# Gated linear attention inside a one-core block: level factors multiplied in place, small levels scored on 32x32 diagonal blocks under one mask, differences taken in pairs, loop written out

## The chip, the cores and the metric

The kernel runs on one core of a Trainium2 chip. A core has TensorE (PE in the profile; PEld is its weight load), VectorE (DVE), ScalarE (ACT), GpSimd (POOL) and SyncE (SP), which run side by side and meet at semaphores. The metric is the device time of one execution in microseconds. The kernel before takes 3309.83 us, the median of 3 runs (3308.33 to 3311.6).

## The reference, cut to what matters

The program is a whole model block (projections, an RWKV-7 mixer, a gated linear attention mixer, an output projection, two feed-forward parts). The change touches the gated linear attention of 4 heads (64 key channels, 128 value channels each) over 1024 tokens, once forward and once backward in time:

```python
def gla_chunked(q, k, v, log_a):
    bc = jnp.cumsum(to_chunks(log_a), axis=-2)
    def step(S, inp):
        o_inter = jnp.einsum('bhcd,bhde->bhce', q_c * jnp.exp(b_c), S)
        diff = b_c[:, :, :, None, :] - b_c[:, :, None, :, :]
        dmat = jnp.exp(jnp.where(mask, diff, -jnp.inf))
        scores = jnp.einsum('bhid,bhjd,bhijd->bhij', q_c, k_c, dmat)
        o_intra = jnp.einsum('bhij,bhje->bhie', scores, v_c)
        S = (S * jnp.exp(b_last[:, :, 0, :])[..., None]
             + jnp.einsum('bhcd,bhce->bhde', k_c * jnp.exp(b_last - b_c), v_c))
        return S, o_inter + o_intra
...
    o_f = gla_chunked(q_h, k_h, v_h, heads(log_a[:, :, 0], GLA_DK))
    o_b = flip(gla_chunked(flip(q_h), flip(k_h), flip(v_h), flip(heads(log_a[:, :, 1], GLA_DK))))
    o = (o_f + o_b).transpose(0, 2, 1, 3)
```

The product over channels with a different decay for every pair of tokens is what makes the scores costly.

## The kernel before

The kernel works on blocks of 128 tokens (BLK), 8 of them (NBLK), with channels on partitions: two tiles of 128 channels (index i) hold two heads each (index par, rows 0 to 63 and 64 to 127). `gla_decay` (L667) writes the running sums of log decays, `sums`, for both directions; `gla_mix` (L735) does the attention; `gla_finish` (L1021) normalises. Each is a block with a barrier at its end.

Inside a block the decay between two tokens is split by the level at which they part: for the levels s = 1, 2, 4, ..., 64 (LEVELS, 7 of them) tokens of one half of a pair of runs of length s look at tokens of the other half, and both are referred to the boundary between them. For a level `level_diff` (L944) writes four differences on DVE (L953 to L956, 128x128 elements each), `level_exp` (L814) exponentiates 128x512 on ACT (L819), DVE multiplies with q and k (L1009), PE forms all four 128x128 score matrices (`scores`, L884, 64 rows of contraction), DVE multiplies them by the 128x128 mask of the level (`masked`, L965), and POOL adds them up (L848, L852). The diagonal is an eighth score. After the last sum PE multiplies with the values (`outputs_of_block`, L893) and DVE adds to `y` (`add_outputs`, L981). The state between blocks runs beside that for both directions: `outputs_of_state` (L907, and the gain at L914) and `next_state` (L975).

All five engines run a loop over the 8 blocks. DVE begins a turn with copies into fixed tiles (L988 to L997) and starts it only when its own last turn and PE's are done, so no work of block j+1 is on DVE, ACT or PE before the outputs of block j are added. Order within an engine is the order of the code; there is no scheduler. Two score buffers and two of each level buffer (`n % 2`) tie level n to level n-2.

Of the kernel before, what the change touches and what calls it, by code (L numbers as in the profile page):

```python
# [34 lines left out]
P = 128  # L35
# [32 lines left out]
for _name, _n in VEC_FIELDS:  # L68
# [7 lines left out]
                ("block_keep", 16), ("gla_diag", 1), ("gla_level", 7)]  # L76
# [11 lines left out]
def constants():  # L88
# [28 lines left out]
    for n, s in enumerate(LEVELS):  # L117
        out[:, CONST["gla_level"] + n] = (p // (2 * s) == j // (2 * s)) & (p // s != j // s)
    out[:, CONST["gla_diag"]] = 2.0 * (p == j)
# [547 lines left out]
def gla_decay(core, dram_const, dram_a_up, lora, sums):  # L667
# [5 lines left out]
    with ExitStack() as ctx:  # L673
# [5 lines left out]
        loaded, products, act_did, dve_did = (core.sem(f"gd_{x}") for x in ("loaded", "products", "act", "dve"))  # L679
# [35 lines left out]
        def _(dve):  # L715
            dve_made.begin(dve)
            dve.wait_ge(loaded, 32)
# [17 lines left out]
def gla_mix(core, dram_const, z, sums, y, room):  # L735

    nc = core.nc
    levels = range(7)  # L740
    scored = ["diag"] + [f"level{n}" for n in levels]
    with ExitStack() as ctx:
# [5 lines left out]
        used = [0]  # L748

        def both(name, tiles, a=1):  # L750

            at = used[0]
            used[0] += tiles * BLK
            own = sb(name, [P, tiles * BLK])[:, :]
            views = (own, room[:, at:at + tiles * BLK])
            if a == 1:
                return [x.rearrange("p (i t) -> p i t", t=BLK) for x in views]
            return [x.rearrange("p (a i t) -> p a i t", a=a, t=BLK) for x in views]

        mask = sb("mask", [P, 8, BLK])  # L760
        summed = sb("summed", [P, 2, 2, BLK])
        summed_d = both("summed_d", 2)
        qk = both("qk", 4, 2)
        v = both("v", 4)
        diff_s = both("diff_s", 4, 2)
        grown_s = both("grown_s", 4, 2)
        qk_s = both("qk_s", 4, 2)
        v_tok = both("v_tok", 4)
        k_tok = both("k_tok", 2)
        state = both("state", 2)  # L770
        diff = sb("diff", [P, 2, 2, 2, BLK])
        grown = sb("grown", [P, 2, 2, 2, BLK])
        qk_l = sb("qk_l", [P, 2, 2, 2, BLK])
        part = sb("part", [P, 2, 4, BLK])
        score = sb("score", [P, 4, BLK])
        ps_score = psum("score", [P, 2, 2, 512])
        ps_v = psum("v", [P, 4, BLK])
        ps_k = psum("k", [P, 4, BLK])
        ps_o = psum("o", [P, 2, 512])
        loaded, zeroed, y_zeroed = core.sem("gm_loaded"), core.sem("gm_zeroed"), core.sem("gm_y_zeroed")  # L780

        def state_steps(d):
            return [f"state0_{d}", f"state1_{d}"]

        def y_steps(d):
            return [f"y0_{d}", f"y1_{d}"]
        dve_steps = ["q_0", "block_sums", "summed_0", "diff_s_0", "q_1", "summed_1", "diff_s_1", "diff_level0"]
        dve_steps += ["qk_s_0", "qk_s_1"]
        for n in levels:
            dve_steps += ([f"diff_level{n + 1}"] if n < 6 else []) + [f"qk_level{n}", f"part_{scored[n]}"]  # L790
            dve_steps += {2: state_steps(1) + y_steps(1), 5: state_steps(0)}.get(n, [])
        dve_steps += ["part_level6"] + y_steps(0)
# [4 lines left out]
        dve_made = Marks(core.sem("gm_dve"), dve_steps)  # L797
        act_made = Marks(core.sem("gm_act"), act_steps)
        pool_made = Marks(core.sem("gm_pool"), [f"sum_{r}" for r in scored[1:]])
        pe_made = Marks(core.sem("gm_pe"), pe_steps)  # L800
        block = ctx.enter_context(nc.Block())

        def tokens(d, j):
# [2302 lines left out]
```

## Time and profile before

| | us |
|---|---|
| median of 3 runs | 3309.83 |
| the profiled execution | 3310.85 |
| its span | 3309.1 |
| of it `gla_mix`, barrier to last add | 248.45 |
| one turn of its loop, from one L988 to the next | 30.3 |
| TensorE busy over the whole span | 91% |
| TensorE busy inside `gla_mix` | 54% |
| DVE busy inside `gla_mix` | 81% |

A line of the timeline gives the start, the duration, the engine, the line, what is written from what, and in brackets how long the engine was idle before and what released it. A duration holds some latency: the next instruction of the same engine can start before it is over, so the difference of two starts is what an instruction costs its queue. An fp32 matmul leaves two records for PE and two for PEld; a transpose leaves one. "big" is the buffer that holds z, y and, before the change, the second copy of several tiles.

### The profile page before, as it was taken

How to read it: one execution, taken by the hardware profiler on the slowest of the kernel's cores; microseconds unless marked ns; L12 is line 12 of the kernel's file. 1: busy time of each engine (PE TensorE's matmuls, PEld its weight loads, DVE VectorE, ACT ScalarE, POOL GpSimd, SP SyncE). 2: the span in 40 equal slices, each digit the busy share in tenths (PEclk: the TensorE clock that was granted, in tenths of full speed). 3: DMA queues.
4: the chain of work that ended last, by engine and by line, in shares of the span. 5: the costliest groups of instructions: out<-in, count | busy, mean ns of one | idle time of the engine just before them, and what ended most of it. 6: DMA issues, size and time to landing. Idle time of an engine off the chain costs nothing.

```text
span 3309.1 us, 55091 instructions
## 1 busy us (share of the span) xinstructions
PE 2995.7 (91%) x23744; PEld 2447.9 (74%) x23744; DVE 1543.4 (47%) x2265; ACT 1169.4 (35%) x1887; POOL 357.9 (11%) x375
## 2 busy tenths in 40 slices
PE   6955559988888879999999999999999999999997
PEld 5844447767787738788888888778787888888886
DVE  4638875433454445443334332666545443334323
ACT  4653335532222124432233232543224333233322
POOL 1003231225444220000000000000000000000000
PEclk8976659998999879999999999999999999999998
DMA  3410004422110013222222223222232222223222
GB/s 125 140 46 0 0 7 154 140 97 57 33 42 14 18 62 103 87 92 96 95 96 90 95 96 108 83 89 89 90 101 83 96 96 96 96 96 121 96 96 82
DMA packets 99137, 273.36 MB, mean 83 GB/s; under 512 B 8160, under 2 KB 35168, under 8 KB 98784
## 3 DMA queue, kind: packets, MB, share of 16 engines
q1 hardware_dynamic: 90128, 237.52, 22.0%
q0 software_dynamic: 8784, 32.51, 2.9%
q8 instruction: 181, 2.97, 0.4%
q14 instruction: 44, 0.36, 0.0%
HBM read 257.42 MB, written 12.58 MB: 82 GB/s over the span
## 4 chain that ended last, share of the span: by engine, by line
PE 59%; DVE 2%; ACT 1%; issue 0%; DMA 0%; DVEq 0%; ACTq 0%
PE be_ps L2696 43%; PE be_ps L2717 14%; PE be_ps L2730 1%; DVE be_ring L2486 1%; PE be_ps L2438 0%; PE be_ps L2432 0%; ACT be_whi L2763 0%; DVE be_raw_r L2869 0%; DMA be_raw<-in_ple_gate 0%; DVE be_total L2451 0%; DVE ext_r L2496 0%; ACT big L2769 0%; DVE big L2459 0%; DVE big L2468 0%; ACT be_ring L2393 0%
## 5 line engine op out<-in xcount | busy, mean ns | idle before, releaser
L2869 DVE TENSOR_TENSOR be_raw_r<-be_raw,be_whi 128x1024 fp32r<-128x1024 f32 x361 | 442.3, 1225 | 993.2 <-ACT be_whi L2763 993.0
L2696 PE MATMUL be_ps<-ext_r,be_whi 128*128 128x512 f32 x2304 | 715.5, 392 | 15.2 <-PEq L2106 8.6
L2763 ACT CAST be_whi<-be_raw 128x1024 fp32r<-128x1024 f32 x361 | 378.8, 1049 | 873.9 <-DMA be_raw<-in_ffn_down 316.3
L2696 PE MATMUL be_ps<-big_r,be_whi 128*128 128x512 f32 x2048 | 642.8, 395 | 2.4 <-DVE big_r L2494 2.4
L2696 PEld LDWEIGHTS be_ps<-ext_r,be_whi 128*128 128x128 f32 x2304 | 433.3, 189 | 108.3 <-issue 10.2
L2696 PEld LDWEIGHTS be_ps<-big_r,be_whi 128*128 128x128 f32 x2048 | 383.9, 188 | 96.8 <-DVE big_r L2494 2.8
L2696 PE MATMUL be_ps<-ext_r,be_raw_r 128*128 128x512 f32 x1152 | 449.9, 391 | 0.0
L2696 PE MATMUL be_ps<-big_r,be_raw_r 128*128 128x512 f32 x1024 | 408.3, 399 | 0.0
L2717 PE MATMUL be_ps<-ext_r,be_whi 128*128 128x512 f32 x1152 | 354.6, 389 | 0.0
L2696 PEld LDWEIGHTS be_ps<-ext_r,be_raw_r 128*128 128x128 f32 x1152 | 217.6, 189 | 45.7
L2717 PEld LDWEIGHTS be_ps<-ext_r,be_whi 128*128 128x128 f32 x1152 | 216.3, 188 | 45.0
L2696 PEld LDWEIGHTS be_ps<-big_r,be_raw_r 128*128 128x128 f32 x1024 | 192.5, 188 | 45.1
L2717 PE MATMUL be_ps<-ext_r,be_raw_r 128*128 128x512 f32 x576 | 224.1, 389 | 0.0
L2717 PEld LDWEIGHTS be_ps<-ext_r,be_raw_r 128*128 128x128 f32 x576 | 108.1, 188 | 22.5
L884 PE MATMUL gm_ps_score<-gm_qk_l 64*128 64x128 f32 x448 | 58.5, 405 | 55.4 <-DVE gm_qk_l L1009 55.4
L2674 POOL DMA_DIRECT2D out<-big x1 | 0.9, 852 | 973.8 <-DVE big L2468 973.8
L884 PEld LDWEIGHTS gm_ps_score<-gm_qk_l 64*128 64x128 f32 x448 | 46.4, 281 | 69.2 <-DVE gm_qk_l L1009 66.5
L2797 ACT CAST ext_r<-be_gate 128x512 fp32r<-128x512 f32 x72 | 44.7, 621 | 142.0 <-DVE be_gate L2890 142.0
L1788 PE MATMUL rw_ps<-rw_x,rw_by_beta 64*64 64x32 f32 x2560 | 92.9, 223 | 1.8 <-ACT rw_x L1671 1.4
L1788 PEld LDWEIGHTS rw_ps<-rw_x,rw_by_beta 64*64 64x64 f32 x2560 | 84.8, 139 | 9.1 <-ACT rw_x L1671 5.0
L2671 POOL DMA_DIRECT2D ext<-in_p x2 | 1.4, 710 | 832.8 <-PE be_ps L2717 832.8
L2791 ACT ACTIVATE be_gate<-be_ps 128x512 f32<-128x512 f32 x88 | 52.7, 599 | 97.5 <-PE be_ps L2696 97.3
(342 smaller groups left out, 4261.3 us busy)
## 6 DMA issues: line engine op xcount, KB each, us to landing
be_raw<-in_ffn_gate SPq DMA_DIRECT2D x88, 512.0 KB, 3.3
be_raw<-in_ffn_up SPq DMA_DIRECT2D x88, 512.0 KB, 3.3
be_raw<-in_ffn_down SPq DMA_DIRECT2D x88, 512.0 KB, 3.3
be_raw<-in_conv_in SPq DMA_DIRECT2D x48, 512.0 KB, 3.3
gp_ada<-in_ada POOLq DMA_DIRECT2D x24, 512.0 KB, 3.6
rp_ada<-in_ada POOLq DMA_DIRECT2D x24, 512.0 KB, 3.7
rwkv_prepared<-big SPq DMA_DIRECT2D x16, 512.0 KB, 3.3
be_raw<-in_w_out SPq DMA_DIRECT2D x16, 512.0 KB, 3.4
```

What stands on the lines that cost most here:

```text
L884: mm = pe.matmul(ps_score[:, n % 2, par, i * BLK:(i + 1) * BLK], src[rows, 1, i], src[rows, 0, i], start=True, stop=True)
L1788: return pe.matmul(out, lhs, moving, start=start, stop=True, skip_group_check=True)
L2486: dve.scalar_tensor_tensor(s.ring[:, i % 2], self.h(i), self.gain(i), self.ps[:, 6] if plan.copy is None else s.kept[:, :], ALU.mult, ALU.mult
L2671: pool.dma_start(p_raw[:, :, cols(half)], a["p"][:, :, cols(half)]).then_inc(p_loaded[half], 16)
L2674: pool.dma_start(out[:, :, cols(0)], big[:, 0:KD, cols(0)]).then_inc(stored[0], 16)
L2696: mm = pe.matmul(ps[:, bank], part[:, k * P:(k + 1) * P], xs(k), start=(k == 0 and i == 0), stop=(k == KD - 1 and i == 2))
L2717: mm = pe.matmul(ps[:, m], part[:, m * P:(m + 1) * P], x, start=(j == 0 and i == 0), stop=(j == NF - 1 and i == 2))
L2730: mm = pe.matmul(ps[:, steps.bank[n, g]], part[:, at], x[:, k, cols(half)], start=(k == 0 and i == 0), stop=(k == 1 and i == 2))
L2763: act.copy(w.hi[:, n % 3], w.raw[:, n % 3]).then_inc(w.hi_ready, 1)
L2791: act.activation(s.gate[:, j % 2, 0:HALF], ps[:, steps.bank[n, 0]], ACT.Silu).then_inc(act_took, 1)
L2797: act.copy(inner(f, j)[0], s.gate[:, j % 2, 0:HALF]).then_inc(a_hi_made, 1)
L2869: dve.tensor_tensor(w.lo(n), w.raw[:, n % 3], w.hi[:, n % 3].bitcast(F32), ALU.subtract).then_inc(w.lo_ready, 1)
```

## The change

- The scaling of q by 0.125 moves out of the loop into `gla_decay`: one DVE instruction of 128x2048.
- The loop over blocks is written out. The copies of q, k, v and of the sums into fixed tiles go; one copy of the sums a block stays and moves to ACT. `exp` of the sums is taken straight from `sums`.
- `level_diff` takes both directions in one instruction: two of 128x256 a level instead of four of 128x128. They go into a ring of 5 slots, are exponentiated in place and multiplied in place.
- The levels 1 to 16 and the diagonal are scored only inside 32x32 diagonal blocks: 16 small matmuls each into one PSUM bank per par, 128x768 masked by one DVE instruction, and folded by three POOL instructions (128x384, 128x128, 128x128). The levels 32 and 64 are scored only where they count (16 and 8 small matmuls), need no mask and stay in PSUM; PE adds the folded low part by a product with the identity (`add_low_scores`), ACT copies the whole (`finish_scores`), PE multiplies with the values (`from_block`).
- The outputs of both directions gather in one PSUM tile; in the first half of the blocks ACT copies them to `y`, in the second half DVE adds them. `y` needs no zeroing.
- The end of block j (low part, high copy, values, outputs) is placed inside block j+1 on PE, ACT and DVE.
- The mask that is loaded shrinks from 128x1024 to 128x384.

The diff, cut to its core:

```diff
-            with dve.Fori(0, NBLK) as j:
-                dve.wait_ge(*dve_made.before(j))
-                dve.wait_ge(*pe_made.before(j))
...
+            def level_diff(j, n):
+                s, to_back = LEVELS[n], 2 * BLK
+                own, out = summed[:, j % 2], ring[:, slot(j, n)]
+                q_out, k_out = out[:, 0], out[:, 1]
+                dve.wait_ge(*act_block.by("summed", j))
+                if j * len(LEVELS) + n >= n_ring:
+                    before, level = ring_user(j, n)
+                    dve.wait_ge(*pe_made.by(f"score{level}", before))
+                middle = by_pair(own, s - 1, to_back + 1, s, 0)
+                dve.tensor_tensor(by_pair(q_out, s, -s, s), by_pair(own, s, to_back - s, s), middle, ALU.subtract)
+                dve.tensor_tensor(by_pair(k_out, 0, s, s), middle, by_pair(own, 0, to_back + s, s), ALU.subtract
+                                  ).then_inc(*dve_made(f"diff{n}"))
...
+            def masked(j):
+                dve.wait_ge(*pe_made.by("score4", j))
+                if j:
+                    dve.wait_ge(*pool_made.by("low", j - 1))
+                dve.tensor_tensor(part.rearrange("p a n t -> p a (n t)"), ps_low[:, :, 0:n_low * 2 * sub],
+                                  mask[:, :].rearrange("p (a t) -> p a t", a=1).to_broadcast([P, 2, n_low * 2 * sub]),
+                                  ALU.mult).then_inc(*dve_made("masked"))
+
+            def next_state(j):
+                dve.wait_ge(*pe_made.by("gain", j))
+                dve.wait_ge(*pe_made.by("from_state", j))
...
+            for j in range(NBLK):
                 level_diff(j, 0)
-                for d in range(2):
-                    dve.wait_ge(*act_made.by(f"exp_s_{d}", j))
+                for d in two:
+                    to_end(j, d)
+                level_diff(j, 1)
+                for d in two:
+                    state_factors(j, d)
                 for n in levels:
+                    if n + 2 < len(LEVELS):
+                        level_diff(j, n + 2)
+                    level_factors(j, n)
+                    if n == 3 and j > NBLK // 2:
+                        add_outputs(j - 1)
+                    if n == 4:
+                        next_state(j)
+                masked(j)
```

```diff
+            def low_scores(place, q, k):
+                for i in two:
+                    for b in range(BLK // sub):
+                        own = slice(b * sub, b * sub + sub)
+                        for par in two:
+                            rows = slice(64 * par, 64 * par + 64)
+                            ins = mm(ps_low[own, par, (place * 2 + i) * sub:(place * 2 + i + 1) * sub], k(rows, i, own), q(rows, i, own))
+                return ins
...
+            for j in range(NBLK):
+                value_tokens(j, 0)
+                own_scores(j)
+                if j:
+                    add_low_scores(j - 1)
+                value_tokens(j, 1)
+                key_tokens(j)
                 scores(j, 0)
-                transposes(j, 1)
                 scores(j, 1)
+                if j:
+                    from_block(j - 1)
+                gains(j)
                 scores(j, 2)
-                outputs_of_state(j, 1)
-                for n in range(3, 8):
-                    scores(j, n)
-                    if n == 5:
-                        outputs_of_state(j, 0)
-                outputs_of_block(j)
+                scores(j, 3)
+                from_states(j)
+                scores(j, 4)
+                scores(j, 5)
+                scores(j, 6)
```

```diff
+            pool.tensor_tensor(part[:, :, 0:3], part[:, :, 0:3], part[:, :, 3:6], ALU.add).then_inc(*pool_made("sum3"))
+            pool.wait_ge(*pool_made.by("sum3", j))
+            pool.tensor_tensor(part[:, :, 0], part[:, :, 0], part[:, :, 1], ALU.add).then_inc(*pool_made("sum1"))
+            pool.wait_ge(*pool_made.by("sum1", j))
+            pool.tensor_tensor(low[:, j % 2], part[:, :, 0], part[:, :, 2], ALU.add).then_inc(*pool_made("low"))
```

On DVE, one level of the middle of a block (s = 4) stood like this before. The four L95x rows are the differences of the next level (s = 8), L1009 the product with q and k, L965 the mask:

```order
L965 TENSOR_TENSOR gm_part<-gm_ps_score,gm_mask 128x512 [waits gm_pe]
L953 TENSOR_TENSOR gm_diff<-gm_summed 128x16x8 [waits gm_act]
L954 TENSOR_TENSOR gm_diff<-gm_summed 128x16x8
L955 TENSOR_TENSOR gm_diff<-gm_summed 128x16x8
L956 TENSOR_TENSOR gm_diff<-gm_summed 128x16x8
L1006 REGISTER_ALU
L1009 TENSOR_TENSOR gm_qk_l<-gm_qk,gm_grown 128x512 [waits gm_pe,gm_act]
```

Each level had this shape, with a mask behind its product. After the change DVE has this from the last level of block 0 to the first product of block 1 (L1024 and L1025 are differences, L1033 those to the end of the block for the state, L1039 the state factors, L1044 a level's product, L1050 the only mask):

```order
L1044 TENSOR_TENSOR gm_ring<-gm_ring,big 128x512 [waits gm_act] x2
L1050 TENSOR_TENSOR gm_part<-gm_ps_low,gm_mask 128x768 [waits gm_pe]
L1024 TENSOR_TENSOR gm_ring<-gm_summed 128x2x128 [waits gm_pe,gm_act_block]
L1025 TENSOR_TENSOR gm_ring<-gm_summed 128x2x128
L1033 TENSOR_TENSOR gm_qk_s<-gla_sums 128x256 x2
L1024 TENSOR_TENSOR gm_ring<-gm_summed 128x2x64x2 [waits gm_pe,gm_act_block]
L1025 TENSOR_TENSOR gm_ring<-gm_summed 128x2x64x2
L1039 TENSOR_TENSOR gm_qk_s<-gm_qk_s,big 128x512 [waits gm_act] x2
L1024 TENSOR_TENSOR gm_ring<-gm_summed 128x2x32x4 [waits gm_pe,gm_act_block]
L1025 TENSOR_TENSOR gm_ring<-gm_summed 128x2x32x4
L1044 TENSOR_TENSOR gm_ring<-gm_ring,big 128x512 [waits gm_act]
```

Of eight masks one is left, and the next block's differences follow it directly.

On PE the middle of a block stood like this before (L884 a level's scores, L907 the products with the state, L914 the gain of the state):

```order
L884 MATMUL gm_ps_score<-gm_qk_l 128x128 x3
L901 REGISTER_ALU [waits gm_act]
L907 MATMUL gm_ps_o<-gm_qk_s,gm_state 128x128 [waits gm_dve]
L907 MATMUL gm_ps_o<-gm_qk_s,gm_state 128x128 x3
L914 MATMUL gm_ps_k<-gm_v_tok,gm_k_tok 64x128 x4
L877 REGISTER_ALU
L880 REGISTER_ALU [waits gm_dve]
L884 MATMUL gm_ps_score<-gm_qk_l 128x128 [waits gm_dve]
```

After the change PE begins block 1 like this (L900 values and L909 keys transposed, L892 all other products; the row that writes `gm_ps_high` from `gm_low` is block 0's `add_low_scores`):

```order
L900 MATMUL gm_ps_v<-const,big 128x128 [waits gm_act]
L900 MATMUL gm_ps_v<-const,big 128x128 x3
L892 MATMUL gm_ps_low<-big 32x32 [waits gm_dve]
L892 MATMUL gm_ps_low<-big 32x32 x15
L892 MATMUL gm_ps_high<-gm_low,const 32x2x32 [waits gm_pe,gm_pool]
L892 MATMUL gm_ps_high<-gm_low,const 32x2x32 x7
L900 MATMUL gm_ps_v<-const,big 128x128 [waits gm_act]
L900 MATMUL gm_ps_v<-const,big 128x128 x3
L909 MATMUL gm_ps_k<-const,gm_qk_s 128x128 [waits gm_dve]
L909 MATMUL gm_ps_k<-const,gm_qk_s 128x128 x3
L892 MATMUL gm_ps_low<-gm_ring 32x32 [waits gm_dve]
L892 MATMUL gm_ps_low<-gm_ring 32x32 x15
```

A level is 16 matmuls instead of 4, and the last block's end stands ahead of this block's second transposes, keys and scores. On ACT, block 1 has this (L847 and L818 exponentials, L827 the copy of block 0's scores, L857 and L861 the transposed values and keys out of PSUM, L832 outputs to `y`):

```order
L847 ACTIVATE gm_qk_s<-gm_qk_s 128x256 [waits gm_dve] x2
L818 ACTIVATE gm_ring<-gm_ring 128x512 [waits gm_dve]
L827 COPY big<-gm_ps_high 128x512 [waits gm_pe_out]
L818 ACTIVATE gm_ring<-gm_ring 128x512 [waits gm_dve]
L857 COPY gm_v_tok<-gm_ps_v 128x512 [waits gm_pe] x2
L861 COPY gm_k_tok<-gm_ps_k 128x512 [waits gm_pe]
L818 ACTIVATE gm_ring<-gm_ring 128x512 [waits gm_dve] x2
L832 COPY big<-gm_ps_o 128x2x2x128 [waits gm_pe_out]
```

The copy of the last block's scores now stands between the first and the second level's exponential; before, ACT had nothing of another block in a turn.

## Rows read from the trace of the kernel before

**Rows 1.** Busy time by stage: `gla_mix`, from barrier to last add.
```profile
core 0: us, PE busy (x) PEld busy (x) DVE busy (x) ACT busy (x) POOL busy (x), PEclk, DMA share, GB/s
242.30:490.75 248.45, 134.77 (x928) 106.39 (x928) 201.75 (x498) 80.19 (x144) 79.36 (x57) 0.60 0.01 2
```

**Rows 2.** Timeline of DVE: first instruction, one turn, the last turn's end.
```profile
247.21 0.29 DVE L988 TENSOR_SCALAR gm_qk<-big 128x256 f32 x1 [3.69 <-DMA gm_mask<-in_const]
...
276.86 0.29 DVE L988 TENSOR_SCALAR gm_qk<-big 128x256 f32 x1 [0.25 <-DVE big L981]
...
277.93 0.42 DVE L997 TENSOR_TENSOR gm_diff_s<-gm_summed_d 128x256 f32<-128x256 f32 x1
278.26 0.29 DVE L988 TENSOR_SCALAR big<-big 128x256 f32 x1
...
288.01 0.68 DVE L1009 TENSOR_TENSOR gm_qk_l<-gm_qk,gm_grown 128x512 f32<-128x512 f32 x1
288.62 0.68 DVE L965 TENSOR_TENSOR gm_part<-gm_ps_score,gm_mask 128x512 f32<-128x512 f32 x1
289.22 0.59 DVE L975 SCALAR_TENSOR_TENSOR big<-big,gm_ps_k 128x128 f32<-128x128 f32 x2
289.73 0.74 DVE L981 TENSOR_TENSOR big<-big,gm_ps_o 128x256 f32 x2
...
307.12 0.29 DVE L988 TENSOR_SCALAR gm_qk<-big 128x256 f32 x1 [0.25 <-DVE big L981]
...
485.62 0.69 DVE L965 TENSOR_TENSOR gm_part<-gm_ps_score,gm_mask 128x512 f32<-128x512 f32 x1 [0.90 <-PE gm_ps_score L884]
490.00 0.75 DVE L981 TENSOR_TENSOR big<-big,gm_ps_o 128x256 f32 x2 [3.69 <-PE gm_ps_o L893]
```

**Rows 3.** Groups by line and shape, DVE, 240 to 491 us: busy, mean ns.
```profile
L955 DVE TENSOR_TENSOR gm_diff<-gm_summed 128x128 f32<-128x128 f32 x56 | 38.3, 684 | 0.0
L954 DVE TENSOR_TENSOR gm_diff<-gm_summed 128x128 f32<-128x128 f32 x56 | 15.8, 282 | 0.0
```

**Rows 4.** Timeline of POOL in the same turn: two of its entries.
```profile
286.39 1.35 POOL L848 TENSOR_TENSOR gm_score<-gm_part 128x512 f32<-128x512 f32 x1 [12.81 <-DVE gm_part L965]
...
292.84 3.86 POOL L852 TENSOR_TENSOR gm_score<-gm_score,gm_part 128x512 f32<-128x512 f32 x2 [2.11 <-DVE gm_part L965]
```

**Rows 5.** Groups by line: a POOL sum of 128x256 in the RWKV mixer.
```profile
L1715 POOL TENSOR_TENSOR rw_e_beta<-big,rw_e_beta 128x256 f32<-128x256 f32 x16 | 11.4, 733 | 0.6
```

**Rows 6.** Timeline of ACT in the same turn: exponential, copy out of PSUM.
```profile
280.74 0.61 ACT L819 ACTIVATE gm_grown<-gm_diff 128x512 f32<-128x512 f32 x1
281.26 0.56 ACT L833 COPY gm_v_tok<-gm_ps_v 128x512 f32<-128x512 f32 x1
```

**Rows 7.** Timeline of PE in the same turn: 64-row and 128-row products.
```profile
288.82 0.72 PE L884 MATMUL gm_ps_score<-gm_qk_l 64*128 64x128 f32 x8 [1.74 <-DVE gm_qk_l L1009]
292.21 1.23 PE L884 MATMUL gm_ps_score<-gm_qk_l 64*128 64x128 f32 x8 [2.67 <-DVE gm_qk_l L1009]
...
303.90 2.07 PE L893 MATMUL gm_ps_o<-gm_score,gm_v_tok 128*128 128x128 f32 x8 [2.30 <-POOL gm_score L852]
```

**Rows 8.** Timeline of PE in the RWKV mixer: 32 records of small products.
```profile
756.10 1.13 PE L1788 MATMUL rw_ps<-rw_masks,rw_beta_end 64*64 64x64 f32 x32 [0.91 <-DVE rw_by_kappa L2012]
...
766.01 1.86 PE L1788 MATMUL rw_ps<-rw_mx,rw_xt 64*64 64x32 f32 x32
...
776.86 1.12 PE L1788 MATMUL rw_ps<-rw_x,rw_by_beta 64*64 64x32 f32 x32
778.28 0.69 PE L1788 MATMUL rw_ps<-rw_masks,rw_beta_end 64*64 64x64 f32 x32 [0.29 <-DVE rw_by_kappa L2012]
```

**Rows 9.** Busy time and clock in stretches of 4 us.
```profile
284.00:288.00 4.00, 3.08 (x34) 2.38 (x33) 3.57 (x9) 1.39 (x3) 1.35 (x1) 0.85 0.00 0
...
756.00:760.00 4.00, 2.42 (x68) 2.10 (x72) 0.58 (x1) 1.35 (x4) 3.85 (x6) 0.50 0.00 0
...
776.00:780.00 4.00, 3.71 (x141) 3.48 (x141) 1.88 (x4) 2.46 (x9) 3.20 (x5) 1.00 0.02 4
```

More of the change, by code:

```diff
@@ L116, in constants @@
             out[:, CONST["level_m"] + 2 * n + d] = np.tile(off | (row == col), 4)
[L117 to L119 removed]
+    row, own = p % 32, np.arange(32)[None, :]
+    low = [(row // (2 * s) == own // (2 * s)) & (row // s != own // s) for s in LEVELS[:5]] + [2.0 * (row == own)]
+    out[:, CONST["gla_low"]:CONST["gla_low"] + 3] = np.concatenate([np.tile(x, 2) for x in low], axis=1).reshape(P, 3, P)
     return out.reshape(P, NCONST * P)
@@ L732, in _, with gla_mix @@
                                            ALU.add).then_inc(*dve_made("scan"))
-def gla_mix(core, dram_const, z, sums, y, room):
+def gla_mix(core, dram_const, z, sums, y):
     nc = core.nc
-    levels = range(7)
-    scored = ["diag"] + [f"level{n}" for n in levels]
+    levels = range(len(LEVELS))
+    low_levels, n_low = range(5), 6
+    n_ring, sub = 5, 32
+    two, heads = range(2), range(4)
     with ExitStack() as ctx:
@@ L760, in gla_mix @@
[L760 to L786, printed above, removed]
@@ L918, in _, with mm, value_tokens @@
-            with pe.Fori(0, NBLK) as j:
-                transposes(j, 0)
+            pe_out.begin(pe)
+            def mm(out, lhs, moving, start=True):
+                return pe.matmul(out, lhs, moving, start=start, stop=True, skip_group_check=True)
+            def value_tokens(j, d):
+                if d:
+                    pe.wait_ge(*act_made.by("v_tok0", j))
+                elif j:
+                    pe.wait_ge(*act_made.by("v_tok1", j - 1))
+                for h in heads:
+                    ins = pe.transpose(ps_v[:, h], z[:, 4 + h, tokens(d, j)], cst(core, "ident"))
+                ins.then_inc(*pe_made(f"v_tok{d}"))
@@ new lines, in from_states @@
+            def from_states(j):
+                pe.wait_ge(*(dve_made.by("state", j - 1) if j else (zeroed, 1)))
+                if j:
+                    pe.wait_ge(y_taken, j)
+                for d in two:
+                    for i in two:
+                        for par in two:
+                            rows = slice(64 * par, 64 * par + 64)
+                            ins = mm(ps_o[:, par, d, i], state[rows, d, i], qk_s[rows, j % 2, d, 0, i], start=(d == 0 and i == 0))
+                ins.then_inc(*pe_made("from_state"))
```

366 lines of the change are left out of this document (188 added, 178 removed).

## The prediction

> **What bounds the kernel now.** First the busy time by stage: the changed stage lasts 248.45 us, with DVE busy 201.75, PE 134.77, ACT 80.19 [rows 1]. So DVE is the engine to cost. Then DVE's timeline: a turn goes from 276.86 to 307.12, 30.3 us [rows 2]. In it DVE is hardly idle until the last mask; then nothing runs on it for about 4 us, because POOL's last sum, PE's product and the addition to `y` come one after the other (the 3.69 in front of L981, seen for the last turn at 490.00) [rows 2]. Third, the groups by shape: L954 and L955 are the same 128x128 subtraction, but L955 takes 684 ns on average where L954 takes 282, which is 38.3 - 15.8 = 22.5 us over the stage [rows 3]. POOL's sum at 286.39 starts just then [rows 4]: DVE waits for it. So a turn is DVE's own work, some 3 us and more that POOL takes from it, and the tail.
>
> **The price of DVE's instructions**, taken as the distance between two starts. 256 elements from two SBUF inputs: 278.26 - 277.93 = 0.33. 512 elements: 288.62 - 288.01 = 0.61, with PSUM as a source the same (289.22 - 288.62 = 0.60). 128 elements of the state's form: two in 289.73 - 289.22 = 0.51, so 0.26 each [rows 2]. From 256 to 512 elements costs 0.28, so 768 elements: 0.61 + 0.28 = 0.89, an estimate from these rows.
>
> **Part by part, DVE of one block after the change.** 14 differences of 256 elements, 14 x 0.33 = 4.6. Two differences to the block's end, 0.7. Two state factors and seven level factors of 512, 9 x 0.61 = 5.5. Four state updates, 1.0. One mask, 0.9. Outputs: 2 x 0.61 in half the blocks, 0.6 on average. Sum 13.3. Gone are the copies, seven of eight masks (each 0.60) and 14 instruction starts of the differences. New strides in the paired form are not seen before; I take 0.33. The bounds: the dense price less a saving that no row suggests, and the full price of 512 elements, 0.61, if a stride halved the rate, which would be 14 x 0.28 = 3.9 more; it is nearest to the dense row, since L954, strided as well, takes its usual 282 ns [rows 3].
>
> **POOL.** Instead of seven sums of 512 there are 384, 128 and 128 elements. 512 take 1.35 [rows 4], 256 take 0.73 [rows 5], so 2.4 ns an element: 1.0, 0.45 and 0.45, 1.9 us, with hand-overs 2.3. DVE loses at most these 1.9 (before, 22.5 / 8 = 2.8 at L955 alone); POOL now starts right behind the mask, among the next block's differences, which all read two SBUF tiles. I take 1.7.
>
> **PE of one block.** A matmul is two records. Seven groups of 16 small matmuls (32 records): the nearest rows are 32 records of 64x64 tiles, 0.69 at full clock and 1.13 at half, and 32 records of a slower arrangement, 1.12 and 1.86 [rows 8] (the clocks are those of the stretches around, 1.00 and 0.50, that is 2.4 and 1.2 GHz [rows 9]). So 4.8 to 7.8 at full clock, 7.9 to 13.0 at half. State products and gains are 32 records of 128 columns, 4 x 0.72 or 4 x 1.23; the value products 8 records, 2.07 at half and about 1.2 at full by the ratio of the other two; three sets of four transposes, at most 0.72 or 1.23 each [rows 7]; the identity products and level 64, half a group each, 0.7 to 1.9. In all 11.7 to 15.0 at full clock, 18.6 to 25.7 at half. Which clock? The stretch 284 to 288, with PE busy 3.08 of 4 us, has 0.85, and the dense small products of the RWKV mixer hold 1.00 [rows 9]; the stage's mean is 0.60 [rows 1]. With the work packed into half the time I take full clock for most of it.
>
> **Waits that remain on DVE.** (a) DVE's state update needs PE's state products, which stand behind level 8's scores. From level 8's factors DVE has only a difference pair and a factor to do, 0.66 + 0.61 = 1.27; PE needs a group (0.69 to 1.12) and 16 records (1.44), about 2.4 with hand-overs. Wait 1.1; at half clock up to 1.86 + 2.46 - 1.27 + 0.2 = 3.2. (b) From the mask the last block's end runs: POOL 2.3, identity product 0.5, copy on ACT 0.6, ACT's next exponential and value copy 1.1, transposes on PE 1.4, key copy 0.6, third exponential 0.6, hand-overs 1: about 8.1 until DVE may multiply level 4 (ACT prices [rows 6]). DVE has for that time 5 difference pairs (3.3), 0.7, two state factors and two level factors (2.4), 6.4, and POOL's 1.7: 8.1. It just covers; I leave 0.4. (c) ACT's copies of outputs in front of an exponential, 0.5. What is queued behind each of these waits is the rest of DVE's block, since DVE is in order.
>
> Block: 13.3 + 1.7 + 1.1 + 0.4 + 0.5 = **17.0 us**.
>
> **Head and tail.** Before, DVE waited 3.69 us for the mask's 512 KB and began at 247.21, 4.9 after the stage's start [rows 2]. 192 KB should land earlier; between no wait (1.2) and the same (4.9) I take 3.0. The tail from the last mask to the end was 490.75 - 485.62 = 5.1; now one mask (0.9), POOL 2.3, identity product 0.6, ACT copy 0.6, value products 1.2 to 2.1 and two additions 1.3: 7.2. The scaling of q lies in `gla_decay`, ahead of everything DVE waits for there; even at 2 us it costs nothing on the path. Sum: 3.0 + 8 x 17.0 + 7.2 - 0.7 (the last block's outputs counted twice) = 145.5. Gain 248.45 - 145.5 = 103. Against the profiled execution's 3310.85, which is 1.0 above the median, that gives 3208; the median should come about 3207.5. The stages around touch no line of this and are taken as unchanged.
>
> **A rule about the shared port.** The row: POOL's sum at 286.39 ran at once and held DVE's L955 for its length; but the pair at 292.84 took 3.86 for two sums of 1.35, so POOL itself waited some 1.1 us while DVE went through four instructions [rows 4]. The Trainium skill, page "SBUF — State Buffer", section "Who interferes with whom", says that a DVE instruction with two SBUF inputs and a GpSimd instruction that reads SBUF exclude each other for a whole instruction, and that the one issued first wins. It doesn't say who is served when both stand in line. Both outcomes agree with it; the second is the rival B below.
>
> **Rivals.**
> A. *Everything covers*: small products at 0.69 and no wait on DVE: 13.3 + 1.0 = 14.3, sum 124, 3186. For it: PE at 11.7 is below that. Against: wait (a) does not go away.
> B. *POOL starves*: behind the mask DVE has 3 pairs, two end differences, two state factors, a level factor, in an unbroken run of 5.1 us with two SBUF inputs each. If POOL gets in only when DVE stops for level 2's exponential, chain (b) begins 5.1 later and DVE stands about 3.5 more. Block 20.5, stage 3.0 + 164 + 6.5 = 173.5: 3236. For it the 292.84 pair; against, that most of POOL's entries waited for nothing.
> C. *PE at half clock becomes the bound*: 18.6 to 25.7 a block, plus about 1: stage 166 to 223, so 3229 to 3285. For it the present 0.60; against, that PE was mostly waiting then.
> D. *Slower than before*: matmuls on neighbouring 32-column tiles do not overlap, so that each record pays more than its start. PE issues 2 x 148 + 12 = 308 records a block. Break-even is (248.45 - 9.5) / 8 = 29.9 us a block, 97 ns a record; if each took as long as a 128-column record at half clock, 1.23 / 8 = 0.154 [rows 7], a block would take 47.4 us and the kernel 3310.85 - 248.45 + 8 x 47.4 + 9.5 = 3451. Against it: the slowest small products seen are 1.86 / 32 = 58 ns [rows 8].
> E. *It doesn't do what it says*: the blocks don't overlap because some semaphore of block j+1 waits for block j's outputs. Then chain (b) and the values stand in the open, some 8 us a block more than 17: 25, stage 209.5, 3272. The order of instructions shows no such wait.
>
> **How the numbers follow.** Forecast 0.52 (3196 to 3224); A 0.12; B 0.13; C 0.18; D 0.02; E 0.02; 0.01 for a case within noise. The measurement can tell about 0.2%, 6.6 us. All but D and the last are faster by more. The range 3186 to 3255 takes in A, the forecast, B and the better half of C, and leaves out about 0.15.
>
> **What would show it.** The stage's length near 145 us; distances between two masks near 17; differences at 0.33 apart; the small groups of 16 matmuls between 0.69 and 1.12 at a granted clock near 1; a wait of about 1 us in front of the state updates; POOL's first sum starting within 1 us of the mask (right) or 4 to 5 behind it (B); PE idle less than a tenth at 0.5 (C). The forecast is wrong if the copy of the high scores on ACT comes so late that DVE waits at level 2 or 4 for several us, or if paired differences cost more than 0.4.

## The result, and the profile after

The changed kernel takes **3234.58 us** (median of 4 runs, 3223.78 to 3236.62); the kernel before, on the same chip, 3310.72 (4 runs). The ratio is 0.9764, with a 95% interval of 0.9741 to 0.9786: faster by 2.4%, inside the range of 3186 to 3255, but 26 us above the 3208 that was forecast. The profiled execution took 3234.0, with a span of 3232.2. It stands within 2 us of what rival B gave (3236), and the trace shows B's mechanism.

The busy time by stage, cut where the stage ends (columns as in [rows 1]):

```profile
core 0: us, PE busy (x) PEld busy (x) DVE busy (x) ACT busy (x) POOL busy (x), PEclk, DMA share, GB/s
242.30:410.00 167.70, 86.30 (x2464) 71.29 (x2464) 109.12 (x249) 70.21 (x153) 49.72 (x24) 0.65 0.01 3
```

Against [rows 1], 248.45 us became 168, DVE's 201.75 busy us became 109.12 and PE's 134.77 became 86.30. DVE is busy 65% of the stage, where it was 81%: it stands idle again. POOL is down by 29.6 only, to 49.72 for 24 instructions, and that is the number to stop at: the three sums of a block were priced at 1.9, and they take 6.2 on average.

One block on DVE, from its mask to the next (L1050 is the mask, L1044 a level's product, L1059 the state updates; last column as in [rows 2]):

```profile
299.62 0.95 DVE L1050 TENSOR_TENSOR gm_part<-gm_ps_low,gm_mask 128x768 f32<-128x768 f32 x1
300.49 0.42 DVE L1024 TENSOR_TENSOR gm_ring<-gm_summed 128x256 f32<-128x256 f32 x1
300.82 0.42 DVE L1025 TENSOR_TENSOR gm_ring<-gm_summed 128x256 f32<-128x256 f32 x1
301.15 0.76 DVE L1033 TENSOR_TENSOR gm_qk_s<-gla_sums 128x256 f32<-128x256 f32 x2
...
305.30 0.43 DVE L1025 TENSOR_TENSOR gm_ring<-gm_summed 128x256 f32<-128x256 f32 x1
309.56 0.69 DVE L1044 TENSOR_TENSOR gm_ring<-gm_ring,big 128x512 f32<-128x512 f32 x1 [3.83 <-ACT gm_ring L818]
...
313.21 0.69 DVE L1044 TENSOR_TENSOR gm_ring<-gm_ring,big 128x512 f32<-128x512 f32 x1 [2.29 <-ACT gm_ring L818]
...
316.53 0.69 DVE L1044 TENSOR_TENSOR gm_ring<-gm_ring,big 128x512 f32<-128x512 f32 x1 [0.68 <-ACT gm_ring L818]
318.02 1.12 DVE L1059 SCALAR_TENSOR_TENSOR gm_state<-gm_state,gm_decay,gm_ps_k 128x128 f32<-128x128 f32 x4 [0.81 <-PE gm_ps_o L892]
319.06 1.29 DVE L1044 TENSOR_TENSOR gm_ring<-gm_ring,big 128x512 f32<-128x512 f32 x2
320.27 0.95 DVE L1050 TENSOR_TENSOR gm_part<-gm_ps_low,gm_mask 128x768 f32<-128x768 f32 x1
```

The block is 320.27 - 299.62 = 20.65 us, of which 3.83 + 2.29 + 0.68 + 0.81 = 7.6 are waits; DVE's own work is 13.04, where 13.3 was forecast. From 300.49 to 305.73 DVE never stops. Now POOL beside it, in this block and in the last one, behind which DVE has nothing to do:

```profile
300.65 5.93 POOL L878 TENSOR_TENSOR gm_part<-gm_part 128x384 f32<-128x384 f32 x1 [13.81 <-DVE gm_part L1050]
306.66 0.45 POOL L880 TENSOR_TENSOR gm_part<-gm_part 128x128 f32<-128x128 f32 x1
307.19 0.45 POOL L884 TENSOR_TENSOR gm_low<-gm_part 128x128 f32<-128x128 f32 x1
...
403.37 0.99 POOL L878 TENSOR_TENSOR gm_part<-gm_part 128x384 f32<-128x384 f32 x1 [13.50 <-DVE gm_part L1050]
```

The same sum of 384 elements has a record of 5.93 us in the first seven blocks (5.92 to 5.93 in each) and of 0.99 in the eighth. The sum itself is not slow: it ends 0.85 us after DVE's run ends (306.58 against 305.73), which is about what it takes alone. So it seems to have waited through the run and only then run; the experiments below test that. Behind it the chain is as the prediction had it. First PE, which waits for POOL (`gm_low`), then ACT, in the same block:

```profile
307.70 0.65 PE L892 MATMUL gm_ps_high<-gm_low,const 32*32 32x64 f32 x16 [6.60 <-POOL gm_low L884]
```

```profile
302.27 0.61 ACT L818 ACTIVATE gm_ring<-gm_ring 128x512 f32<-128x512 f32 x1
308.42 0.59 ACT L827 COPY big<-gm_ps_high 128x512 f32<-128x512 f32 x1 [5.53 <-PE gm_ps_high L892]
308.90 0.63 ACT L818 ACTIVATE gm_ring<-gm_ring 128x512 f32<-128x512 f32 x1
```

ACT's copy of the last block's scores is queued ahead of the second level's exponential, so DVE waits for an exponential whose input, the differences at 301.82 and 302.16, it had finished by 302.58, 6.3 us before that exponential starts at 308.90. The list of waits sums it up for the stage (us in total, times, longest):

```profile
PE gm_ps_high L892 <- POOL gm_low L884: 47.9, 8, 6.6
DVE gm_ring L1044 <- ACT gm_ring L818: 45.5, 18, 3.8
DVE gm_state L1059 <- PE gm_ps_o L892: 4.9, 8, 1.3
```

Read alone, the second line says that ACT is late. ACT was waiting for PE, PE for POOL, and POOL for DVE itself: DVE waits for its own unbroken run.

Behind the stage nothing changed by design, but the RWKV mixer's 2560 products took 383.2 us from first to last start against 377.2 before. The eleven kernels of the experiments below, none of which touches them, have 375.2 to 383.6 there, so this is a run's own scatter. The stage gave 80.6 us (the first product behind it starts at 411.6 instead of 492.2); the mixer took 6.0 back and the rest of the kernel gave 2.3, so that the profiled execution shows only 76.9. In the experiments I therefore read the stage by that start, called the marker, first and the total second.

### The profile page after: what moved, and what is told of

Its sections match the earlier page's. It is cut to its first block, busy times and chain, and to the rows that moved or that the text cites. A ratio compares the mean times of both kernels' runs of the same rounds, so it can differ in the third digit from the quotient of the medians.

```text
span 3232.2 us, 57142 instructions
## 1 busy us (share of the span) xinstructions
PE 2949.1 (91%) x25280; PEld 2417.1 (75%) x25280; DVE 1451.8 (45%) x2017; ACT 1159.3 (36%) x1896; POOL 328.1 (10%) x342
## 3 DMA queue, kind: packets, MB, share of 16 engines
q1 hardware_dynamic: 90128, 237.19, 22.4%
## 4 chain that ended last, share of the span: by engine, by line
PE 60%; DVE 2%; ACT 1%; issue 0%; DMA 0%; DVEq 0%; ACTq 0%
PE be_ps L2767 44%; PE be_ps L2788 15%; DVE be_ring L2557 1%; PE be_ps L2801 1%; PE be_ps L2509 0%; PE be_ps L2503 0%; ACT be_whi L2834 0%; DVE be_raw_r L2940 0%; DMA be_raw<-in_ple_gate 0%; DVE be_total L2522 0%; DVE ext_r L2567 0%; ACT big L2840 0%; DVE big L2530 0%; DVE big L2539 0%; ACT be_ring L2464 0%
## 5 line engine op out<-in xcount | busy, mean ns | idle before, releaser
L1477 PE MATMUL rp_acc<-xn_hi,rp_whi 128*128 128x512 f32 x240 | 78.1, 407 | 4.7 <-PEq L1097 4.7
L1859 PE MATMUL rw_ps<-rw_mx,rw_xt 64*64 64x32 f32 x2048 | 77.0, 225 | 4.0 <-DVE rw_mx L2125 1.6
```

The source lines that it names most:

```text
L1477: ins = pe.matmul(acc[:, s % 2, hf * HALF:(hf + 1) * HALF], part[:, s % 2, k], x[:, k, hf * HALF:(hf + 1) * HALF], start=(k == 0 and part ...
L1859: return pe.matmul(out, lhs, moving, start=start, stop=True, skip_group_check=True)
```

## The experiments

The theory: POOL's sum can't start beside a DVE instruction with two inputs in SBUF, and DVE, which always has the next one at hand, is served first. Rivals: the sum is simply slow next to other traffic; ACT's order is at fault; PE is the bound. Each ratio is to the kernel before, measured again in the same series (3304.09 to 3306.7); since that differs from the 3310.72 above, medians of different series are compared by ratio or by the marker. Line numbers shift a little from version to version.

**1. State updates behind the mask.** Their inputs are the state and PE's PSUM, so only one tensor in SBUF.

```diff
-            dve_steps += {4: ["state"], 6: ["masked"]}.get(n, [])
+            dve_steps += {6: ["masked", "state"]}.get(n, [])
...
-                    if n == 4:
-                        next_state(j)
                 masked(j)
+                next_state(j)
```

> Edit: in the changed kernel the four state updates of a block (one SBUF tensor, one PSUM tensor each, 1.04 us together) move from behind level 16's factors to behind the mask; nothing is added or left out. Theory (POOL's first sum of 384 elements takes 5.93 us because it waits until DVE ends its run of instructions with two SBUF inputs): POOL gets in at once, its sum takes about 1.0 us, what hangs on it comes 4.9 us earlier, a block takes 16 to 17.5 us instead of 20.6, and the kernel 3201 to 3215. Rival (the sum is slow for another reason, such as a late release or a slow form of 384 elements): it stays near 5.9 us and the kernel near 3234.

Measured: 3183.45 us (3180.17 to 3185.99), 0.9624 of before [0.9608, 0.964]; the stage is 43.6 us shorter than with the change alone (marker 368.0 against 411.6). DVE and POOL behind a mask:

```profile
313.83 0.96 DVE L1050 TENSOR_TENSOR gm_part<-gm_ps_low,gm_mask 128x768 f32<-128x768 f32 x1 [0.56 <-PE gm_ps_low L892]
314.70 1.11 DVE L1059 SCALAR_TENSOR_TENSOR gm_state<-gm_state,gm_decay,gm_ps_k 128x128 f32<-128x128 f32 x4
315.73 0.42 DVE L1024 TENSOR_TENSOR gm_ring<-gm_summed 128x256 f32<-128x256 f32 x1
316.07 0.67 DVE L1025 TENSOR_TENSOR gm_ring<-gm_summed 128x256 f32<-128x256 f32 x1
...
314.86 1.00 POOL L878 TENSOR_TENSOR gm_part<-gm_part 128x384 f32<-128x384 f32 x1 [13.07 <-DVE gm_part L1050]
315.94 0.52 POOL L880 TENSOR_TENSOR gm_part<-gm_part 128x128 f32<-128x128 f32 x1
```

The sum takes 0.99 to 1.00 us in all eight blocks, the updates beside it keep their usual length (1.11 against 1.12), and a block falls to 14.8 on average (15.04 in the last ones). The DVE work is the same to the instruction. Two waits went at once: POOL's chain, and the one for PE's state products (4.9 us in the stage), which now have until after the mask. The second is one reason why the kernel came out 18 us below the expected 3201; experiment 11 keeps that wait and gains less. No other version measured here has a lower median, though experiment 10 can't be told from it.

**2. The three sums on DVE** (L878, L880, L884 moved from POOL behind the mask, else as the changed kernel).

> Edit: the three sums that fold the low scores (384, 128 and 128 elements) run on DVE behind the mask instead of on POOL. Theory (the port wait is what makes the block 20.6 us): DVE pays 0.47 + 0.20 + 0.20 = 0.9 us and three hand-overs, some 1.2 in all, the chain to the next block's level 2 is 5 to 6 us shorter, a block takes 16 to 17 us, the kernel 3198 to 3212. Rival (DVE's own work is the bound of the block): each microsecond put on DVE makes it slower, 8 x 1.2 = 10 us more, 3244.

Measured: 3193.21 (3190.91 to 3204.86), 0.9663 [0.964, 0.9686]; marker 379.2, block 16.2 on average (15.3 to 16.8). The sums take 0.56, 0.29 and 0.29 us on DVE:

```profile
322.59 0.56 DVE L1038 TENSOR_TENSOR gm_part<-gm_part 128x384 f32<-128x384 f32 x1
323.19 0.29 DVE L1040 TENSOR_TENSOR gm_part<-gm_part 128x128 f32<-128x128 f32 x1
```

Work put on the engine that was thought to be the bound makes the stage 32.4 us shorter than in the changed kernel; by the ratios the kernel gains 33 us. The median lies 5 us below the range expected. With POOL out of the stage nothing has to wait for DVE's run to end, so this and the first experiment agree, by different edits.

**3. Differences unpaired**: the change with the four 128-element differences of before instead of the two paired ones.

> Edit: in the changed kernel the differences of a level are again four instructions of 128x128 elements instead of two of 256. Theory (the run of DVE instructions behind the mask is on the path, since POOL waits for its end): three levels lie in that run and each costs 4 x 0.20 - 2 x 0.335 = 0.14 us more, others are covered in part by DVE's waits; 0.5 to 1.0 us a block, the kernel 4 to 8 us slower, 3238 to 3242. Rival (no part of DVE's work is on the path, ACT and PE are): within 1 us of 3234.

Measured: 3233.78 (3226.99 to 3238.68), 0.9772 [0.9751, 0.9793], which can't be told from the change and by itself would speak for the rival. But the stage is 5.0 us longer (marker 416.6), as the theory has it; the mixer, with 378.1 against 383.2 us, hides that in the total. POOL's sum is 6.47 us in seven blocks and 0.99 in the last: its length follows that of DVE's run (5.78 us instead of 5.24) and not its own work. Pairing is worth about 5 us here.

**4. Before, with its loop written out and nothing else.**

```diff
-            with dve.Fori(0, NBLK) as j:
+            for j in range(NBLK):
```

(on all four engines)

> Edit: the kernel before with its loop over 8 blocks written out on all engines, with every wait kept as it was. Theory (writing the loop out buys nothing by itself, it only lets other blocks' work be placed): the turn loses ACT's table load, which DVE does not wait for, and about 0.25 us at its start; 3305 to 3310. Rival (the loop's registers and branches hold the engines up): 1 us a turn or more, 3302 or less.

Measured: 3302.75 (10 runs, 3293.91 to 3308.77) against 3306.35, 0.9986 [0.9975, 0.9996]; the stage lost 7.3 us, 0.9 a turn. That is nearer to the rival's 1 us a turn than to the theory's 0.25: the loop did cost something. Even so it is under a tenth of the 80.6; the rest is the work taken away and the overlap.

**5. DVE waits for POOL's first sum.** One wait added to the changed kernel:

```diff
                 masked(j)
...
+                dve.wait_ge(*pool_made.by("sum3", j))
```

> Edit: in the changed kernel, DVE waits behind its mask until POOL's first sum is done; nothing is moved, added or left out. Theory (the sum is held up by DVE's own run): a wait that costs DVE about 1.2 us a block takes 4.9 us off the sum; a block takes 15.7 to 16.6 us instead of 20.6, the kernel 3190 to 3205. Rival (the gain of moving the state updates came from where the updates stand, that is from PE's state products no longer being waited for): the sum may be short, but the kernel gains no more than the 1.0 us a block that this wait had, less 1.2 for the new wait: 3232 or more.

Measured: 3199.46 (3195.08 to 3209.16), 0.9689 [0.9666, 0.9712]; marker 384.0, so 27.6 us less in the stage than in the changed kernel, with blocks of 16.7. The kernel's time is where the theory put it.

```profile
306.68 0.95 DVE L1050 TENSOR_TENSOR gm_part<-gm_ps_low,gm_mask 128x768 f32<-128x768 f32 x1
308.74 0.42 DVE L1024 TENSOR_TENSOR gm_ring<-gm_summed 128x256 f32<-128x256 f32 x1 [1.11 <-POOL gm_part L878]
...
307.71 0.99 POOL L878 TENSOR_TENSOR gm_part<-gm_part 128x384 f32<-128x384 f32 x1 [14.36 <-DVE gm_part L1050]
```

A wait of 1.11 us a block on the busiest engine of the stage makes it 27.6 us shorter, and POOL's sum takes 0.99 in all eight blocks. This excludes that the sum is slow by itself or hindered by ACT and PE, whose work is unchanged; the wait for PE's state products is still there (5.4 us in the stage), so the gain isn't due to that one either.

**6. Each small score matmul issued twice** (base: experiment 1; the second writes the same again).

```diff
-                for i in two:
+                for i in (0, 1) * 2:
```

> Edit: on top of the kernel with the state updates behind the mask (3183.45), PE computes each group of 16 small products of the levels 1 to 16 and the diagonal twice, to the same place. Theory (PE is not the bound; two of its groups, levels 8 and 16, lie on what DVE waits for): a group costs 0.35 us, 6 of them 2.1 us of PE a block, of which 0.3 to 0.7 reach the path: 3186 to 3189. Rival (PE's small products set the pace): all 2.1 us show, 17 us, 3200.

Measured: 3203.74 (3200.83 to 3211.15), 0.9699 [0.968, 0.9719]: the stage is 19.0 us longer than in experiment 1, 2.4 a block. I had expected PE to have room, and the time is what the rival gave (3200): DVE's wait in front of the mask grew from 0.6 us in the stage to 14.1. But part of it is not PE's work. In the waits of PE:

```profile
PE gm_ps_low L892 <- issue: 12.5, 14, 1.9
PE gm_ps_high L892 <- issue: 7.3, 5, 1.7
```

PE stood 19.8 us with nothing that the profile names to wait for, with at most 1.0 of it in the base. The doubled stream shows this, and the trace doesn't say why. So the experiment says that PE has less than a doubled load of slack, and can't size it.

**7. The end of a block in its own turn** (base: experiment 1; `add_low_scores`, `finish_scores`, `from_block` and the outputs of block j no longer stand in block j+1).

> Edit: on top of the kernel with the state updates behind the mask (3183.45), the end of block j (identity product, copy of the high scores, value products, outputs) stands at the end of block j on PE, ACT and DVE instead of inside block j+1. Theory (half of the gain of the change is this placement): POOL's sums, the identity product, ACT's copy, the value products and the outputs, 6 to 7 us, are in the open, less what DVE has ready of the next block (two difference pairs and two end differences, 2 us): a block takes 19 to 20.5 us instead of 15.0, the kernel 3218 to 3228. Rival (waits on semaphores let the engines run ahead whatever the order): within 5 us of 3183.

Measured: 3207.99 (3207.51 to 3216.27), 0.9708 [0.9691, 0.9724]; marker 393.8, block 18.4, so 25.8 us over experiment 1. The chain is in the open, in front of the state factors in one half of the blocks (below) and of the outputs' addition in the other:

```profile
319.12 1.29 DVE L1033 TENSOR_TENSOR gm_qk_s<-gm_qk_s,big 128x512 f32<-128x512 f32 x2 [4.34 <-ACT gm_qk_s L847]
```

The direction was as expected, the size 10 to 20 us smaller. Even so the stage is 17.8 us shorter than in the changed kernel with its deferral: deferring pays (25.8 us here) only if the chain isn't held up by what it is laid beside.

**8. ACT's order** (base: experiment 1; value copy 0 first, the third and the fifth level's exponential each ahead of a copy), against the 0.56 and 0.68 us that DVE still waits for ACT.

> Edit: on top of the kernel with the state updates behind the mask (3183.45), ACT copies the first value tile out of PSUM before it exponentiates the state's factors, exponentiates level 4 before it copies the keys, and level 16 before it copies the outputs. Theory (three waits of DVE for ACT and PE, 0.56, 0.68 and 0.56 us a block, come from ACT's order): 1.0 to 1.8 us a block go, the kernel 3169 to 3176. Rival (PE's clock and order hold the same waits in place): within 3 us of 3183.

Measured: 3187.74 (3185.15 to 3189.22), 0.9646 [0.963, 0.9662]; marker 373.6, so 5.6 us more in the stage. The 1.0 to 1.8 us a block that were expected didn't go, and the kernel came out 4 us slower, a little beyond what the rival allows. DVE's waits for ACT fell from 5.8 us in the stage to 1.5, but a wait in front of the mask took their place, 9.1 us where there had been 0.6:

```profile
302.98 0.96 DVE L1053 TENSOR_TENSOR gm_part<-gm_ps_low,gm_mask 128x768 f32<-128x768 f32 x1 [1.85 <-PE gm_ps_low L895]
```

**9 and 10. The gains behind the last level's scores on PE**, on the kernel of experiment 8 (9) and of experiment 1 (10), to see what that new wait consists of. The gains, 16 matmuls of 128 columns, had stood ahead of the second level's scores.

```diff
-        pe_steps = ["v_tok0", "diag", "v_tok1", "k_tok", "score0", "score1", "gain", "score2", "score3", "from_state",
-                    "score4", "score5", "score6"]
+        pe_steps = ["v_tok0", "diag", "v_tok1", "k_tok", "score0", "score1", "score2", "score3", "from_state",
+                    "score4", "gain", "score5", "score6"]
```

> Base is the run with ScalarE's order changed (3187.5 profiled, block 14.9, DVE waits 1.18 to 1.85 us for the last level's scores on TensorE before each mask). Here the 16 matmuls of the gains (1.5 to 2.0 us of TensorE) are issued behind the scores of the last level instead of ahead of the second level's. Theory 'TensorE is dense from the keys to the last scores': the mask's wait for PE falls under 0.4 us, the block to 13.8 to 14.2 us, the kernel to 3174 to 3182. Rival 'the wait only moves to the state updates behind the mask, which need the gains': a new DVE wait of 0.8 to 1.5 us at the state updates, block 14.7 to 15.0, kernel 3185 to 3190.

> The same move of the gains, on the kernel with only the state updates behind the mask (ScalarE's order unchanged; 3180.2 profiled, block 15.0, waits per block 0.56 and 0.68 for ScalarE's exponentials and 0.56 for PE). Theory: only the 0.56 us for PE can go, 4.5 us in eight blocks: 3175 to 3180. Rival 'the wait moves to the state updates': 3180 to 3186.

Measured: 3188.34 (3182.39 to 3191.81), 0.9647 [0.9627, 0.9668], and 3185.45 (3183.8 to 3187.29), 0.9636 [0.9617, 0.9654]. In both the time is the one that the rival gave. The markers are 370.1 and 373.1. In 9 DVE has now:

```profile
315.87 0.96 DVE L1053 TENSOR_TENSOR gm_part<-gm_ps_low,gm_mask 128x768 f32<-128x768 f32 x1 [0.90 <-PE gm_ps_low L895]
317.42 1.12 DVE L1062 SCALAR_TENSOR_TENSOR gm_state<-gm_state,gm_decay,gm_ps_k 128x128 f32<-128x128 f32 x4 [0.59 <-PE gm_ps_k L895]
```

The mask waits 4.7 us in the stage instead of 9.1, the state updates 6.3 instead of nothing. In 10 my premise was off as well: the base had a wait in front of the mask in one block only (0.6 us), so there was nothing to take. In 10 the mask waits in all eight blocks, 2.6 us together, and the updates 5.5. At 15 us a block PE seems as late as DVE: in 9 its `from_block` still takes 2.07 us for 8 records, the half-clock price of [rows 7], and the gains up to 1.97. Giving PE less work between the keys and the last scores wasn't tried.

**11. One state update behind the mask**: the changed kernel with three updates where they were and the fourth behind the mask. It asks how little POOL needs.

```diff
-            dve_steps += {4: ["state"], 6: ["masked"]}.get(n, [])
+            dve_steps += {6: ["masked", "state"]}.get(n, [])
...
+                        next_state(j, [(0, 0), (0, 1), (1, 0)])
...
                 masked(j)
+                next_state(j, [(1, 1)])
```

> The changed kernel (3234, block 20.7, POOL's first sum 5.93 us), with three of the four state updates where they were and only the last one moved behind the mask. It is one instruction of 0.26 us with one input in SBUF, between the mask and the next run of instructions with two. Theory 'any such instruction lets POOL's queued sum in': POOL's first sum at about 1.0 to 1.6 us in most blocks, kernel 3195 to 3205. Rival 'the gap is too short or comes before POOL's request (0.17 us behind the mask)': the sum still takes about 5.9 us, kernel 3230 to 3236.

Measured: 3195.71 (3193.02 to 3199.09), 0.9663 [0.9644, 0.9683]; marker 380.6, 31.0 us less than the changed kernel.

```profile
306.59 0.34 DVE L1058 SCALAR_TENSOR_TENSOR gm_state<-gm_state,gm_decay,gm_ps_k 128x128 f32<-128x128 f32 x1
306.85 1.18 DVE L1024 TENSOR_TENSOR gm_ring<-gm_summed 128x256 f32<-128x256 f32 x1
307.95 0.67 DVE L1025 TENSOR_TENSOR gm_ring<-gm_summed 128x256 f32<-128x256 f32 x1
...
306.75 0.99 POOL L878 TENSOR_TENSOR gm_part<-gm_part 128x384 f32<-128x384 f32 x1 [13.19 <-DVE gm_part L1050]
307.83 0.52 POOL L880 TENSOR_TENSOR gm_part<-gm_part 128x128 f32<-128x128 f32 x1
```

One instruction of 0.26 us is enough: the sum takes 0.99 to 1.00 us in all eight blocks, seven of which have DVE's run behind the update. The kernel is in the range that the theory gave. Once POOL's sum has begun, the difference at 306.85 is held for its length: 1.18 instead of 0.42. That makes the price of the sums on DVE readable: 0.76 + 0.25 + 0.26 = 1.3 us a block here, where they meet differences, and 0.5 in experiment 1, where the first meets the state updates. The rest of the 12.6 us to experiment 1 is the wait for PE's state products (5.8 us in the stage), which here stands ahead of the three updates as before.

## Why the prediction was right and wrong

**Right in the price of DVE's work.** Costing by DVE's instruction starts held: a difference of 256 elements is 0.335 (taken as 0.33, so the new strides cost nothing) and the mask 0.87 (0.89). A block's DVE work is 13.04 in the blocks where ACT takes the outputs and 14.15 where DVE adds them, 13.5 on average (13.3). The head was 245.24 - 242.3 = 2.9 (3.0), the tail from the last mask to 410.2 was 7.9 (7.2). Rivals D and E are out: small products run far below 97 ns a record, and the blocks overlap. In C one bound was added up wrongly: the terms that give 11.7 us of PE at full clock give 19.7 at half, not 18.6.

**The step that failed is wait (b).** The prediction laid the last block's end, 8.1 us, beside 6.4 us of DVE's work plus 1.7 of POOL's share, and found that "it just covers". The cover was the very thing that kept the chain from starting. Its first link didn't run beside those instructions, so the 5.2 us of DVE's run and the chain came one after the other: waits of 3.83 and 2.29 in place of 0.4, and nothing in place of the 1.7 that POOL was to take. That is 4.0 of a block; DVE's work and wait (a) gave 0.5 back in the block shown, and wait (c) took 0.2: 20.65 against 17.0. The seven blocks from mask to mask are 20.66 on average, so this makes 25.6 us. The first had been counted like the others, but has no last block's end in it: its mask starts 12.5 us after the first difference (257.73 - 245.24), 4.5 less than 17.0. With 0.7 more in the tail and the forecast's correction of 0.7, which has no counterpart when the stage is cut at the masks, the stage comes to 22.4 us above the 145.5, as measured (167.9). The rest of the 26 lies outside the stage: 6.0 more in the RWKV mixer, less elsewhere. Rival B shares the error of the first block (173.5 against 167.9), so that its total hit to 2 us is partly luck; its mechanism and its 20.5 a block are not. (Its 5.1 us of run need four pairs of differences, as the trace has them; three were listed.)

**The evidence was weighed wrongly.** Rival B had the mechanism, the run of 5.1 us and the block of 20.5 in it, but a chance of 0.13, since most of POOL's entries before had waited for nothing [rows 4]. Those entries met another DVE stream, with masks, copies and waits in it. The clearest row with POOL queued against consecutive DVE instructions, the pair at 292.84, spoke for B, and the change made just that the normal case. The kernel before even shows what ends such a wait. The first sum of that pair has a record of 2.38 us where the sums that ran alone in that turn have 1.26 to 1.27, so it waited 1.1, until about the mask at 294.02, which has one input in PSUM; and the difference behind the mask was then held:

```profile
293.42 0.68 DVE L1009 TENSOR_TENSOR gm_qk_l<-gm_qk,gm_grown 128x512 f32<-128x512 f32 x1
294.02 0.67 DVE L965 TENSOR_TENSOR gm_part<-gm_ps_score,gm_mask 128x512 f32<-128x512 f32 x1
294.62 0.75 DVE L953 TENSOR_TENSOR gm_diff<-gm_summed 128x128 f32<-128x128 f32 x1
```

The Trainium skill, page "SBUF — State Buffer", section "Who interferes with whom", has a VectorE instruction with two SBUF inputs and a GpSimd instruction that reads SBUF exclude each other. The 1.18 us of L1024 in experiment 11 and POOL's 5.93 agree with it in the two directions. For the question on which the case turned, who is served when both stand in line, the changed kernel's answer is DVE, as long as its next instruction is ready. Why POOL at 286.39 was served at once in the kernel before, ahead of L955, stays open; no run isolates it. It isn't the form of the differences alone, since experiment 3 has the same four a level and its sum was held for the whole run.

**One sign was worded badly.** I had said that B would show as POOL's first sum *starting* 4 to 5 us behind the mask. Its record starts 0.08 us behind the mask, and the wait is inside the record. By my own test B would have looked refuted. The sign is the duration, 5.93 against 0.99.

**PE's small groups were mis-sized.** 32 records were taken as 0.69 to 1.12 at full clock; they take 0.35 (297.19 in the rows below), and 64 records 0.76 (at 295.41), or 0.89 at a granted clock of 0.50 (291.16). The nearest rows, in the RWKV mixer, were not near. It cost the forecast little, since PE's work set only wait (a), and C is refuted in its size: PE's busy time is 10.8 us a block, not 18.6 to 25.7, at a mean granted clock of 0.65.

```profile
291.16 0.89 PE L892 MATMUL gm_ps_low<-gm_ring 64*32 64x32 f32 x64
291.98 2.07 PE L892 MATMUL gm_ps_o<-big,gm_v_tok 128*128 128x128 f32 x8
...
297.19 0.35 PE L892 MATMUL gm_ps_low<-gm_ring 64*32 64x32 f32 x32
```

Nor did full clock come "for most of it". In stretches of 4 us:

```profile
286.00:290.00 4.00, 1.39 (x20) 1.15 (x21) 1.24 (x3) 1.59 (x3) 0.77 (x2) 0.50 0.00 0
290.00:294.00 4.00, 4.00 (x80) 3.38 (x78) 1.71 (x5) 2.22 (x4) 0.00 (x0) 0.50 0.02 4
294.00:298.00 4.00, 3.55 (x129) 3.10 (x128) 2.36 (x7) 3.91 (x10) 0.00 (x0) 0.89 0.02 4
```

PE waits about 6.6 us for POOL in nearly each block, resumes at 1.2 GHz (0.50), and is granted 2.4 GHz only within the third stretch. In experiment 1, with 83.82 busy us in 124.30 instead of 86.30 in 167.70, the mean is 0.73 against 0.65: the idle time that POOL caused seems to have cost clock too; no run isolates it.

**Waits (a) and (c)** were 0.81 and 0.68 (1.1 and 0.5), the right size.

## What to carry to other kernels

When a small GpSimd step starts a chain, look at what VectorE runs beside it: in this kernel an unbroken stream of instructions with two SBUF inputs didn't cover the step, it postponed it, and one instruction with a single SBUF input, put right behind the producer, let it in. Work that lies "beside" other work is free only if both can run together, so put the reason for that next to every cover. And when a wait names an engine, follow it to the end: here VectorE's wait for ScalarE led over TensorE and GpSimd back to VectorE.

## What the runs showed of the hardware

- A GpSimd sum that was ready 0.1 us behind its mask was held for the whole of a VectorE run, in seven blocks of seven: 5.93 us with 5.2 of run, 6.47 with the 5.8 of experiment 3, 0.99 with none. An update of 0.26 us with one SBUF and one PSUM tensor let it in, in the seven blocks of seven where a run followed (experiment 11).
- State updates with one tensor in SBUF and one in PSUM ran at their usual length (1.11 us for four) beside a GpSimd sum; differences with both inputs in SBUF were held for all of it (1.18 instead of 0.42).
- Matmuls on 64x32 tiles: 32 records in 0.35 us; 64 records in 0.69 us from their first start to the next group's (295.41 to 296.10), some 11 ns a record.
- A doubled stream of small matmuls (experiment 6) left TensorE idle for 19.8 us with no named cause, up to 1.9 us at a time.
